# A first norm done tile by tile, rotary halves swapped by DMA, and the step sizes' chain cut into pieces beside the attention heads

## The reference

```python
h = rms_norm(x, norm_mix_w, 1e-6)              # 512 x 1024
q, k, v, z, xbc, dt_raw, gate_a, gate_s = split(h @ w_in)
q, k = apply_rotary(q), apply_rotary(k)        # 8 heads, two halves of 64 each
# apply_rotary: [t1*cos - t2*sin, t2*cos + t1*sin], t1, t2 the 32-wide parts of each 64
att = diff_attention(q, k, v, lam)             # softmax(q1 k1) - lam * softmax(q2 k2), times v
dt = softplus(dt_raw + dt_bias); a = -exp(a_log)      # 32 heads of the SSD branch
y = ssd_chunked_scan(xs * dt, dt * a, B, C)    # uses exp of cumulative sums of dt * a
x = x + merged(att, ssd) @ w_out
x = x + hierarchical_moe(...)                  # 64 experts, all their weights are read
# the second layer follows: four kinds of attention and an MLP
```

## Time and profile before

| what | value |
|---|---|
| median of 3 runs | 2699.12 us (2692.74 to 2705.61) |
| the profiled execution's own time | 2695.84 us |
| its span | 2694.5 us |
| TensorE busy | 2345.8 us, 87% |
| VectorE / ScalarE / GpSimd busy | 967.6 / 707.8 / 351.8 us |
| mean granted clock of TensorE | 0.961 of full speed |

### The profile page before, as it was taken

The page is one execution under the profiler, slowest core; times in us unless marked ns, Lnnn a source line. Parts: engine busy times, 40 slices in busy tenths (PEclk is TensorE's granted clock), DMA queues, the critical chain, the costliest instruction groups (busy, mean ns, idle before and its releaser), DMA issues.

```text
span 2694.5 us, 31496 instructions
## 1 busy us (share of the span) xinstructions
PE 2345.8 (87%) x12676; PEld 1701.8 (63%) x12676; DVE 967.6 (36%) x1943; ACT 707.8 (26%) x1365; POOL 351.8 (13%) x455
## 2 busy tenths in 40 slices
PE   5998899999989996998787887887759978999999
PEld 4666677777778854554444444444437756788887
DVE  4555656756632224111010100001016567442432
ACT  4444445544532100000000000000013347232231
POOL 1111122221210011111111111111103110000000
PEclk9999899999999997999999999999989978999999
DMA  6122032223243447999999999999981201122221
GB/s 149 47 58 65 20 94 63 78 67 106 79 162 135 171 156 313 425 425 425 425 425 424 425 425 425 425 424 425 426 352 65 78 24 40 63 94 94 94 94 63
DMA packets 141300, 562.29 MB, mean 209 GB/s; under 512 B 13936, under 2 KB 74644, under 8 KB 116576
## 3 DMA queue, kind: packets, MB, share of 16 engines
q1 hardware_dynamic: 124144, 528.23, 49.6%
q0 software_dynamic: 16288, 28.98, 3.1%
q10 hardware_dynamic: 720, 3.01, 0.3%
HBM read 553.85 MB, written 31.46 MB: 217 GB/s over the span
## 4 chain that ended last, share of the span: by engine, by line
PE 40%; DMA 27%; DVE 3%; issue 1%; ACT 1%; POOL 0%; POOLq 0%; DVEq 0%; ACTq 0%; SPq 0%
DMA ringx<-in_w_expert_gate 15%; DMA ringx<-in_w_expert_up 9%; PE ps L630 9%; PE ps L632 9%; PE ps L631 9%; PE ps L969 6%; PE ps L883 2%; PE ps L989 2%; DMA ringx<-in_w_expert_down 2%; PE ps L623 1%; PE ps L1096 1%; PE ps L1118 1%; DVE s L2225 0%; PE ps L1106 0%; PE ps L1144 0%
## 5 line engine op out<-in xcount | busy, mean ns | idle before, releaser
L2072 DVE TENSOR_TENSOR hid<-ps,sg 128x256 f32<-128x256 f32 x64 | 27.2, 425 | 836.6 <-issue 818.8
L630 PE MATMUL ps<-hTh,hb 128*128 128x512 f32 x704 | 310.9, 442 | 4.2 <-DVE ringr L1654 4.2
L969 PE MATMUL ps<-ringx,gxT 128*64 128x256 f32 x2080 | 253.4, 395 | 56.7 <-DMA ringx<-in_w_expert_up 44.3
L632 PE MATMUL ps<-hTh,ringr 128*128 128x512 f32 x704 | 284.7, 404 | 0.0
L631 PE MATMUL ps<-hTl,hb 128*128 128x512 f32 x704 | 283.9, 403 | 0.0
L969 PEld LDWEIGHTS ps<-ringx,gxT 128*64 128x64 f32 x2080 | 170.1, 136 | 145.9 <-issue 88.0
L1460 ACT COPY ys<-ps 128x512 f32<-128x512 f32 x64 | 37.5, 586 | 629.8 <-PE ps L989 629.8
L969 PE MATMUL ps<-ring,gxT 128*64 128x256 f32 x1344 | 161.0, 390 | 36.0 <-DMA ring<-in_w_expert_up 22.1
L1654 DVE TENSOR_TENSOR ringr<-ring,hb 128x1024 fp32r<-128x1024 f32 x112 | 136.7, 1224 | 94.4 <-ACT hb L1230 93.9
L969 PEld LDWEIGHTS ps<-ring,gxT 128*64 128x64 f32 x1344 | 109.4, 134 | 95.2 <-issue 60.1
L630 PEld LDWEIGHTS ps<-hTh,hb 128*128 128x128 f32 x704 | 138.8, 197 | 45.9 <-issue 19.3
(11 more groups left out here) (455 smaller groups left out, 4135.3 us busy)
## 6 DMA issues: line engine op xcount, KB each, us to landing
ringx<-in_w_expert_up SPq DMA_DIRECT2D x43, 2048.0 KB, 41.2
ringx<-in_w_expert_gate SPq DMA_DIRECT2D x22, 2048.0 KB, 41.3
ringx<-in_w_expert_down SPq DMA_DIRECT2D x22, 2048.0 KB, 40.9
ring<-in_w_expert_down SPq DMA_DIRECT2D x21, 2048.0 KB, 41.0
ring<-in_w_expert_gate SPq DMA_DIRECT2D x21, 2048.0 KB, 41.3
ring<-in_w_expert_up SPq DMA_DIRECT2D x21, 2048.0 KB, 41.2
ringy<-in_w_expert_down SPq DMA_DIRECT2D x21, 2048.0 KB, 40.9
ringy<-in_w_expert_gate SPq DMA_DIRECT2D x21, 2048.0 KB, 41.3
```

The source lines that it names most:

```text
L630: pe.matmul(o, lh, rh, start=start and n == 0, stop=False)
L632: m = pe.matmul(o, ll, rh, start=False, stop=stop and n == len(ks_) - 1)
L969: m = pe.matmul(b[c * 64:c * 64 + 64, 0:256].rearrange("p (n j) -> p n j", j=2), gxTs[e % 2][:, k % 4, k // 4 * 64:k // 4 * 64 + 64], w4[: ...
```

## The change

1. **First norm tile by tile.** X comes as four transfers, each with a semaphore of its own; square, rsqrt, scaling, transposes and both halves go tile by tile. The norm's weight is no longer applied as a column behind the transposes but as a row (`nrow`, broadcast to 128 partitions by a transfer of 512 KB on ScalarE's queue) ahead of them. On SP's queue the weights' first three chunks follow X at once; the rest of the constants stands behind chunk 0, the small vectors behind chunk 2. Their transposes (`pe_vectors`) move behind head 0, the cosine's chain between steps 1 and 2 of head 0.
2. **Heads' halves.** `pe_perm` goes. When raw is there, SP sends four transfers of 32 partitions (64 KB each) from raw to a buffer (`pqs`, which are ang and rn), swapped; the sign is in the sine. `dve_rope` multiplies that buffer by sin instead of bank 2.
3. **Step sizes' chain.** `steps_setup` now has six parts, called in heads 5 to 7 at n = 34, 36, ..., 44 of `merged(49, 28)`, behind the head's step. Behind head 7 come the value transposes and `merged(13, 9)` with group 0 alone.

```diff
     ident, mhalf = cc("ident"), cc("mhalf")
+
+    early = cat["tri"][0]
     region_a = PM.at
-    X = sb("X", [128, NT, D])
+    hTl = sb("hTl", [128, 8, S], F32R)
     XN = sb("XN", [128, NT, D])
     hTh = sb("hTh", [128, 8, S], F32R)
     attT = sb("attT", [128, 8, S])
-    hTl = over("hTl", [128, 8, S], F32R, region_a)
+    X = over("X", [128, NT, D], F32, region_a + 49152)
...
+    pqs = [ang, rn]
+    nrow_mix = over("nrow", [128, D], F32, work0 + 65152)
...
+    def sp_chunk(i):
+        width, pieces = mix[i]
+        for c0, n, src in pieces:
+            dst = cols3(ring[i % RING], src.shape[1], width)[:, :, c0:c0 + n]
+            sp.dma_start(dst, src).then_inc(s[f"ring{i % RING}"], 16)
+
+    def sp_halves(h):
+
+        for j in range(2):
+            sp.wait_ge(*at("raw", 3 * h + j + 1))
+            if h == 0:
+                sp.wait_ge(*at("ang", 2))
+            for c in range(0, 128, 32):
+                o = c + 32 if c % 64 == 0 else c - 32
+                sp.dma_start(pqs[j][c:c + 32, :], raws[j][o:o + 32, :]).then_inc(s[("halfq", "halfk")[j]], 16)
+
     def sp_first():
-        sp.dma_start(X[:, :, :], t["x"].rearrange("a (n p) d -> p (a n) d", p=128)).then_inc(s["x"], 16)
+        xr = t["x"].rearrange("a (n p) d -> p (a n) d", p=128)
+        for tt in range(NT):
+            sp.dma_start(X[:, tt, :], xr[:, tt, :]).then_inc(s[f"xa{tt}"], 16)
+        for i in range(RING):
+            sp_chunk(i)
+            if i == 0:
+                sp.dma_start(C[:, early:ncc], t["consts"][:, early:ncc]).then_inc(s["consts"], 16)
...
+        for i in range(RING, len(mix)):
+            if i < RING + 8:
+                sp_halves(i - RING)
+            sp.wait_ge(*mix_used(i - RING))
+            sp_chunk(i)
...
     def pe_start():
+        pe.wait_ge(*at("ident", 16))
+        for tt in range(NT):
+            pe.wait_ge(*at("xn", tt + 1))
+            for i in range(2):
+                b = bank(2 * tt + i)
+                pe_turn4(b, lambda k: XN[:, tt, (i * 4 + k) * 128:(i * 4 + k) * 128 + 128]).then_inc(s["xT"], 1)
+                held[2 * tt + i] = at("htl", 2 * tt + i + 1)
+        pe.wait_ge(*at("htl", 8))
+
+    def pe_vectors():
         pe.wait_ge(*at("consts", 16))
-        pe.wait_ge(*at("vecs", 384))
+        pe.wait_ge(*at("vecs", 368))
         b = bank(7)
         pe.transpose(b[:, 0:nrow], vrow[:, :], ident[0:nrow, 0:nrow])
         pe.transpose(b[:, nrow:nrow + 128], crow[:, :], ident).then_inc(s["vt"], 1)
         held[7] = at("vcol", 1)
-        for k in range(8):
-            b = bank(k)
-            for tt in range(NT):
-                if k == 0:
-                    pe.wait_ge(*at("xn", tt + 1))
-                m = pe.transpose(b[:, tt * 128:tt * 128 + 128], XN[:, tt, k * 128:k * 128 + 128], ident)
...
-    def pe_perm(h, j):
-        b = bank(2)
-        pe.wait_ge(*at("raw", 3 * h + j + 1))
-        pe.matmul(b[:, :], cc("perm"), raws[j][:, :], start=True, stop=True).then_inc(s["perm"], 1)
-        held[2] = at("rope", 2 * h + j + 1)
...
-        if step in (4, 6):
-            pe_perm(h, step // 2 - 2)
...
     def act_start():
-        a.dma_start(C[:, :], t["consts"]).then_inc(s["consts"], 16)
-        a.wait_ge(*at("x", 16))
-        for tt in range(NT):
-            m = a.activation(XN[:, tt, :], X[:, tt, :], ACT.Square, scale=1.0 / 32, accum_out=st[:, 8 + tt:9 + tt])
-        m.then_inc(s["ssq"], 1)
-        a.wait_ge(*at("vcols", 1))
-        for k in range(8):
-            a.wait_ge(*at("xT", k + 1))
-            a.activation(hTh[:, k, :], banks[k][:, :], ACT.Copy, scale=col("norm_mix_w", k)).then_inc(s["hth"], 1)
-        a.wait_ge(*at("htl", 8))
+        a.dma_start(C[:, 0:early], t["consts"][:, 0:early]).then_inc(s["ident"], 16)
+        a.dma_start(nrow_mix[:, :], t["norm_mix_w"].to_broadcast([128, D])).then_inc(s["nrow"], 16)
+        for tt in range(NT + 1):
+            if tt < NT:
+                a.wait_ge(*at(f"xa{tt}", 16))
+                a.activation(XN[:, tt, :], X[:, tt, :], ACT.Square, scale=1.0 / 32,
+                             accum_out=st[:, 8 + tt:9 + tt]).then_inc(s[f"ssq{tt}"], 1)
+            if tt > 0:
+                for i in range(2):
+                    a.wait_ge(*at("xT", 2 * tt - 2 + i + 1))
+                    a.copy(hTh[:, i * 4:i * 4 + 4, (tt - 1) * 128:tt * 128],
+                           banks[2 * tt - 2 + i][:, :].rearrange("p (k c) -> p k c", k=4)).then_inc(s["hth"], 1)
         for n in range(3):
             act_hi(n)
         a.wait_ge(*at("lam", 1))
         a.activation(st[:, 2:4], st[:, 0:2], ACT.Exp).then_inc(s["lame"], 1)
-        for i, dst in enumerate((sinT, cosT)):
-            a.wait_ge(*at("ang", i + 1))
-            a.activation(dst[:, :], dst[:, :], ACT.Sin).then_inc(s["rot"], 1)
+        act_sine(0)
...
+        v.wait_ge(*at("ident", 16))
+        v.wait_ge(*at("nrow", 16))
+        for tt in range(NT + 1):
+            if tt < NT:
+                v.wait_ge(*at("rs1", tt + 1))
+                v.scalar_tensor_tensor(XN[:, tt, :], X[:, tt, :], st[:, 12 + tt:13 + tt], nrow_mix[:, :], MUL,
+                                       MUL).then_inc(s["xn"], 1)
+            if tt > 0:
+                for i in range(2):
+                    ks_, ts = slice(i * 4, i * 4 + 4), slice((tt - 1) * 128, tt * 128)
+                    v.wait_ge(*at("hth", 2 * tt - 2 + i + 1))
+                    v.tensor_tensor(hTl[:, ks_, ts], banks[2 * tt - 2 + i][:, :].rearrange("p (k c) -> p k c", k=4),
+                                    hTh[:, ks_, ts], SUB).then_inc(s["htl"], 1)
         for n in range(2):
...
     def dve_rope(h, j):
         dst = (qs, ks)[j][h % 2]
-        v.wait_ge(*at("perm", 2 * h + j + 1))
         if h >= 2 and j == 0:
             v.wait_ge(*at("sc", 8 * h - 8))
-        vs(v.tensor_tensor(dst[:, :], raws[j][:, :], cosT[:, :], MUL))
-        vs(v.tensor_tensor(raws[j][:, :], banks[2][:, :], sinT[:, :], MUL))
-        v.tensor_tensor(dst[:, :], dst[:, :], raws[j][:, :], ADD).then_inc(s["rope"], 1)
+        v.wait_ge(*at("raw", 3 * h + j + 1))
+        v.tensor_tensor(dst[:, :], raws[j][:, :], cosT[:, :], MUL)
+        v.wait_ge(*at(("halfq", "halfk")[j], 64 * h + 64))
+        vs(v.tensor_tensor(pqs[j][:, :], pqs[j][:, :], sinT[:, :], MUL))
+        v.tensor_tensor(dst[:, :], dst[:, :], pqs[j][:, :], ADD).then_inc(s["rope"], 1)
...
+        if part == 2:
             v.wait_ge(*at("dte", 1))
             vs(v.tensor_scalar(s3, s2, 2.0, None, ADD))
             vs(v.reciprocal(s3, s3))
             vs(v.tensor_tensor(s2, s2, s3, MUL))
             vs(v.tensor_tensor(s3, s2, s2, MUL))
             vs(v.tensor_scalar(d, s3, 2.0 / 17, 2.0 / 15, MUL, ADD))
-            for c in (13, 11, 9, 7, 5, 3, 1):
+        if part in (2, 3, 4):
+            for c in ((13, 11), (9, 7, 5), (3, 1))[part - 2]:
                 vs(v.tensor_tensor(d, d, s3, MUL))
                 vs(v.tensor_scalar(d, d, 2.0 / c, None, ADD))
+        if part == 4:
             vs(v.tensor_tensor(d, d, s2, MUL))
...
         for step in range(7):
             dve_head(0, step)
+            if step == 1:
+                dve_angles(1)
+            if step == 3:
+                v.wait_ge(*at("rot", 2))
+        dve_vectors()
         for side, n in merged(49, 28):
             if side == 0:
                 dve_head(1 + n // 7, n % 7)
+                if n >= 34 and n % 2 == 0:
+                    dve_steps_setup((n - 34) // 2)
             else:
                 dve_attention(n)
-        for side, n in merged(16, 9):
+        for side, n in merged(13, 9):
             if side == 1:
                 dve_attention(28 + n)
-            elif n < 3:
-                dve_steps_setup(n)
             else:
-                dve_group(0, n - 3)
+                dve_group(0, n)
...
     def pool_first():
+        g.dma_start(posi[:, :], t["positions"].to_broadcast([128, S])).then_inc(s["bcast"], 16)
         for name, n in SCALARS:
             g.dma_start(scv(name), t[name].to_broadcast([128, n])).then_inc(s["bcast"], 16)
-        g.dma_start(posi[:, :], t["positions"].to_broadcast([128, S])).then_inc(s["bcast"], 16)
         g.dma_start(wdt[:, :, :], wview("w_in", 9216, 32)).then_inc(s["wdt"], 16)
-        g.wait_ge(*at("consts", 16))
-        g.wait_ge(*at("ssq", 1))
-        pool_rstd(st[:, 12:16], st[:, 8:12], 1e-6, "rs1")
+        g.wait_ge(*at("ident", 16))
+        for tt in range(NT):
+            g.wait_ge(*at(f"ssq{tt}", 1))
+            pool_rstd(st[:, 12 + tt:13 + tt], st[:, 8 + tt:9 + tt], 1e-6, "rs1")
```

More of the change, by code:

```diff
@@ L75, in constants @@
     put("ones", 1.0)
-    perm = np.zeros((128, 128))
-    for m in range(128):
-        if m % 64 < 32:
-            perm[m + 32, m] = -1.0
-        else:
-            perm[m - 32, m] = 1.0
-    put("perm", perm)
     dist = p[:, None] + 384 - np.arange(512)[None, :]
```

110 lines of the change are left out of this document (51 added, 59 removed), and 22 rows, old and new, of tables (AFTER, SEMS).

## The result

The changed kernel took 2684.42 us (median of six runs, 2679.73 to 2689.81), the kernel before beside it 2699.24 (2692.74 to 2705.61): a ratio of 0.995 with the 95% interval 0.993 to 0.9969. The time is inside the wide range of the prediction (2655 to 2688), though not inside its own range for the forecast (2662 to 2678), and the sign is right, but the saving is 14.8 us where 26 to 29 were forecast (26.2 by the sum, 29 by 2670 against the median). The profiled execution took 2679.73 us.

A forecast was written before the change was run, and what follows sets the result against it. The weight stream bounds 1000 to 2100 us; savings lie in the first matmul's path, the heads and their end. -11.1 + 0.6 - 8.8 - 1.0 - 0.7 - 5.2 = -26.2 from 2695.8 gives 2670 us; own range 2662 to 2678, wide 2655 to 2688.

The forecast's parts named there:

- Everything behind the heads shifts rigidly: After the heads, all stages, the weights' stream too, were to start earlier by the full saving, 26.2 us.
- First norm and vectors: Kernel start: first projection matmul at 25.1 us, -11.1; the vectors' transposes behind head 0 cost +0.6.
- Halves: Eight heads: q permutations removed -8.8 us, head 0's k permutation -1.0, VectorE's passes -0.7; transfers covered by softmax work.
- k permutations inside the heads: In the heads VectorE has no gap, so removing k permutations saves only in head 0, -1.0 us, apart from head 7's.
- Chain: Step sizes' chain moved into heads 5 to 7: -26.4 at the heads' end, +14.3, +1.1, +2.8 and +3 back, -5.2 us.
- Nothing makes this shorter in head 5: Head 5: the 8.7 us from scores until VectorE has the weights ready would stay, part of the chain's +14.3 us.
- Group 0's interleaving: Group 0 with attention pieces 28 to 36 in 13 steps: TensorE waits for copies, +3 us, between 0 and 8.
- head 7's k permutation: End of the heads: its removal was counted within the chain's -26.4 us, not with the halves.
- Rival (b): Kernel start gives less, as the broadcast lands late or X's tiles come no sooner; group 0 costs 8: 2675 to 2684; 0.20.
- (d): No change: chain in heads 5 to 7 costs more than it gave, start gives 6; within 13 us of before; 0.07.
- (a): Heads and chain: everything removed is saved and the chain wholly hidden, -46.8 us, 2649 us; chance 0.13.
- (c): Heads: halves arrive late and VectorE waits in the rope; at 16 us each, +54, about 2750 us; chance 0.04.

The follow-up runs named there:

- experiment 4: Kernel before and changed kernel, both with unread matmuls ahead of two TensorE waits in each SSD group, on one chip: 2690.75 and 2667.36 us.
- the kernels with the fillers: Kernels given 12 unread matmuls per SSD group ahead of two TensorE waits (7 and 5); the changed kernel so altered took 2666.55 us.
- experiment 7's first kernel: Changed kernel with the step sizes' chain back behind the heads, VectorE's polynomial one slot too late, no unread matmuls: 2685.16 us.
- experiment 10: Changed kernel with VectorE's first chain piece, the split of the step sizes' weights, after head step 31 instead of 34: 2671.87 us.
- experiment 12: Changed kernel with unread matmuls, weights split after step 31, last chain piece and sums three steps later, group 0 spread over 16 slots: 2654.15 us.
- experiment 9: Changed kernel with the halves' swap back on TensorE as permutation matmuls, chain still in pieces, no unread matmuls: 2694.59 us.
- experiment 3: Changed kernel with unread matmuls ahead of two TensorE waits in each SSD group, 7 and 5: 2666.55 us.
- experiment 7's mended kernel: Changed kernel with unread matmuls ahead of both waits and the chain behind the heads in its exact old places: 2672.44 us.
- experiment 1: Changed kernel run again unchanged for a second profile: 2682.22 us.
- the first wait alone: Changed kernel with seven unread matmuls ahead of only the first of the two TensorE waits in each SSD group: 2660.39 us.

## Why the prediction was off

The step that failed is the last of the sum: "Everything behind the heads shifts rigidly". Up to the end of group 0 the changed kernel's lead was 23.2 us of the forecast 26.2; then it became 15.3, because TensorE's granted clock in groups 1 to 5 was 0.94 throughout, and in the kernel before 1.00 at first. That the clock took it is shown by the pair of experiment 4: kept up in both kernels, the lead is 24.1 at the mark and 23.4 at the end. I had read the half clock as the price of long stalls (5.6 us for da) and took the groups to run in the new kernel as they ran in the old. No row of mine showed them: the earlier trace rows has 36.12 to 360 us and 1000 to 2100 us, and groups 1 to 6 lie between. The Trainium skill (TensorE: Matmul & The Clock Gate, Part 1) says, of a kernel's beginning, that the number of slow matmuls varies from run to run. In the middle of this kernel the traces agree: groups 4 and 5 of the kernel before took 54.6 us in one profile and 53.0 in the other. It belonged into the range as a case of its own, of 3.2 us for each of some six groups.

That the time still fell between 2655 and 2688 was luck: no term of the sum, and none of the rivals, had this loss.

The terms, by the kernels with the fillers (end of group 0; medians in brackets, not all measured side by side):

- *First norm and vectors*, forecast -10.5 (-11.1 + 0.6): 341.88 to 331.16, **-10.7** (-11.2). Right, but partly by luck. The pieces listed behind X's landing add up to 9.3 us and not to the 8.8 that were used, so that the term should have been -10.6 and the whole sum -25.7. X was on time. The weights' first chunk came 1.3 us later than needed, where I had it off the path.
- *Halves*, forecast -10.5 (-8.8 - 1.0 - 0.7): 331.16 to 322.68, **-8.5** (-6.7). The mechanism held: TensorE waits longer for bk, and k permutations inside the heads save nothing. The size is 2 to 4 too high, of which the extra half clock in one head (30.6 for 28.2 us) may be the most; I have not shown that. The transfers held TensorE by no more than the 1.2 us of head 0.
- *Chain*, forecast -5.2: 322.68 to 317.35, **-5.3** (-5.9), and 1.7 by experiment 7's first kernel; the forecast is not refuted. Its parts came: 7.4 us for wdl, then 8.26 for the matmuls at 0.66, 20.44 us from scores to scores (20.7 forecast). "Nothing makes this shorter in head 5" held for this order alone: VectorE's part 0 three steps earlier removed the wait and gave 10.4 us (experiment 10). Group 0's interleaving was 1.2 in experiment 12 (3 forecast): the wait for xs (4.7 instead of 2.0) is mostly paid for by shorter ones in head 7.
- *What the terms left out*: they are not independent. I put head 7's k permutation into the chain's term. The chain's move shows its gain only with the permutations gone; with them in, group 0 ended 2.2 us later (331.16 to 333.39), no gain within what the marks can tell.

Rival (b), a start that gives less, did not happen, though its time was near (2675 to 2684). Nor did (d), whose time was near too: the chain cost no more than it gave. (a) and (c) are out. The forecast's 26.2 would have been right within 3 us for a kernel whose groups hold the full clock.

What stays open is why the periods go to 54.6 and how soon. The groups' instructions are the same in all kernels. Where group 0's issue stood at 363.8, 373.6 or 376.1 us (experiment 10, the changed kernel and its repetition), every period was 54.6. At 377.5 us (experiment 7's first kernel) the first and the last of six were 53.0. At 388.4 us (experiment 9) they were 51.4, 53.0, 54.6, 54.6, 54.6 and 53.0, and at 396.7 us (the kernel before) 51.4, 51.4, 53.0 and then 54.6. That speaks for the moment at which the groups begin, but a mere delay was not tried.

The clock also varies behind the groups. From SyncE's last ssdh issue to the end of the span passed 1941.9 us in the profile of experiment 3 and 1957.0 in that of experiment 7's mended kernel, both with the groups at full clock. So single executions say little about a few microseconds.

## What to carry to other kernels

When a change moves a long, regular stretch without touching it, look at the granted clock of its single periods first: if one program shows two lengths for the same instructions, a shift may change the mix, and a saving is only measured where this is pinned. Short waits in an otherwise busy TensorE can be worth filling with matmuls nobody reads: seven in a wait of 1.9 us in each group saved 18.9 us here by the marks (experiment 1 against the first wait alone; 2682 and 2660 in the medians, which were not measured side by side). And when an edit is undone for a test, look at the waits of the undone kernel against those of the original: the misplaced piece stood there as 9.45 for 5.6 us.

## What the runs showed of the hardware

- TensorE at half clock follows waits as short as 1.88 us, and not always: the same wait was followed by full clock at 330.88 and by half clock at 493.07 in one execution. Without fillers a group's period takes the values 51.4, 53.0 and 54.6 us. With 12 matmuls more ahead of the waits it was 51.9 each time.
- Runs of one kernel spread with the mean granted clock: the changed kernel had spans from 2665.6 us (0.964) to 2691.2 (0.952). With the groups at full clock they still spread: experiment 7's mended kernel took 2663.32 to 2683.57 us.
- A 64 KB transfer within SBUF lands 2.0 us after its issue, and four are issued in 2.5 us.
- A broadcast of 512 KB to 128 partitions landed in 7.1 us on ScalarE's queue at the start, where the other one, on GpSimd's queue, had taken 15.9.
